# A hybrid decoder layer with PEER experts on one core: gathered rows broadcast by GpSimd, V sums over three PSUM banks, token weights in a zeroed wide row

## What is computed

```python
def _peer(h, wq, keys, u_tab, v_tab):                 # 288 tokens, width 2048
    q = (tb @ wq).reshape(TOK_BLOCK, PEER_HEADS, 2, PEER_DK)
    s = jnp.einsum('thpd,hpkd->thpk', q, keys)
    sv, si = lax.top_k(s, PEER_TOPK)
    ...                                               # the best 16 sums of two: eid (128 experts of a token), g (their weights)
    hid = jax.nn.gelu(jnp.einsum('td,ted->te', tb, u_tab[eid]), approximate=False)
    return jnp.einsum('te,ted->td', (g * hid), v_tab[eid])
```

## Time and profile before

| | |
|---|---|
| median of three runs | 2301.0 us |
| the profiled execution, its time | 2297.46 us |
| its span | 2295.3 us |
| TensorE (PE) busy | 2200.6 us, 96% |
| weight loads (PEld) busy | 1941.9 us, 85% |
| VectorE (DVE) busy | 1664.9 us, 73% |
| ScalarE (ACT) busy | 925.3 us, 40% |
| GpSimd (POOL) busy | 387.8 us, 17% |
| HBM traffic | 675.03 MB, mean 294 GB/s |
| chunks of gathered tokens run from, to | 1033 us to 2050 us |

### The profile page before, as it was taken

The page is one execution under the profiler, slowest core; times in us unless marked ns, Lnnn a source line. Parts: engine busy times, 40 slices in busy tenths (PEclk is TensorE's granted clock), DMA queues, the critical chain, the costliest instruction groups (busy, mean ns, idle before and its releaser), DMA issues.

```text
span 2295.3 us, 38685 instructions
## 1 busy us (share of the span) xinstructions
PE 2200.6 (96%) x14916; PEld 1941.9 (85%) x14916; DVE 1664.9 (73%) x3097; ACT 925.3 (40%) x1080; POOL 387.8 (17%) x336
## 2 busy tenths in 40 slices
PE   6899999779989999999999999999999999999996
PEld 2399888548979989999988888889888898989996
DVE  1269777434456699878888787887877878877686
ACT  1332323353353227644434444344343443444444
POOL 1044000300000008201122222222212322111000
PEclk9999999889999999999999999999999999999998
DMA  9977776976754445788899999998999999988863
GB/s 377 384 264 293 266 267 241 359 288 269 254 180 128 148 147 236 254 305 285 293 339 352 346 370 355 355 367 326 360 364 339 359 356 359 345 314 305 282 206 128
DMA packets 157366, 675.03 MB, mean 294 GB/s; under 512 B 17328, under 2 KB 17712, under 8 KB 134032
## 3 DMA queue, kind: packets, MB, share of 16 engines
q1 hardware_dynamic: 122112, 444.65, 54.2%
q0 software_dynamic: 33648, 219.49, 24.8%
q10 hardware_dynamic: 1440, 8.56, 0.9%
HBM read 650.68 MB, written 21.95 MB: 293 GB/s over the span
## 4 chain that ended last, share of the span: by engine, by line
PE 80%; DVE 8%; DMA 8%; ACT 2%; issue 1%; SPq 0%; DVEq 0%; POOL 0%; ACTq 0%
PE vb L1619 16%; PE zb L1604 14%; PE vb L1621 6%; PE zb L1606 6%; PE zb L531 5%; PE zb L533 5%; PE zb L532 5%; DMA ada_first<-in_w_ada 3%; PE vb L1653 3%; PE vb L1643 3%; PE vb L1584 2%; DMA raw<-in_v 2%; PE vb L1247 2%; DVE lo L484 2%; PE zb L1560 1%; PE zb L1247 1%
## 5 line engine op out<-in xcount | busy, mean ns | idle before, releaser
L475 ACT ACTIVATE hi<-raw 128x1024 fp32r<-128x1024 f32 x624 | 659.9, 1059 | 978.2 <-PE vb L1619 284.3
L484 DVE TENSOR_TENSOR lo<-raw,hi 128x1024 fp32r<-128x1024 f32 x624 | 765.7, 1231 | 276.2 <-ACT hi L475 267.9
L1604 PE MATMUL zb<-act_hl,hi 128*128 128x416 f32 x1792 | 556.5, 368 | 0.0
L1619 PE MATMUL vb<-w_rest,hi 128*128 128x416 f32 x1536 | 495.4, 368 | 0.0
L1606 PE MATMUL zb<-act_hl,lo 128*128 128x208 f32 x1680 | 435.6, 259 | 0.0
L1604 PEld LDWEIGHTS zb<-act_hl,hi 128*128 128x128 f32 x1792 | 335.1, 188 | 35.9 <-issue 27.7
L1621 PE MATMUL vb<-w_rest,lo 128*128 128x208 f32 x1280 | 329.9, 258 | 0.0
L1606 PEld LDWEIGHTS zb<-act_hl,lo 128*128 128x128 f32 x1680 | 320.8, 191 | 5.1
L1619 PEld LDWEIGHTS vb<-w_rest,hi 128*128 128x128 f32 x1536 | 288.8, 188 | 1.1
L531 PE MATMUL zb<-act_hl,hi 128*128 128x288 f32 x960 | 287.2, 299 | 0.0
L532 PE MATMUL zb<-act_hl,hi 128*128 128x288 f32 x960 | 282.5, 294 | 0.0
(11 more groups left out here) (291 smaller groups left out, 2759.1 us busy)
## 6 DMA issues: line engine op xcount, KB each, us to landing
raw<-in_v SPq DMA_DIRECT2D x256, 512.0 KB, 6.4
raw<-in_u SPq DMA_DIRECT2D x224, 512.0 KB, 6.4
raw<-in_w_in SPq DMA_DIRECT2D x80, 512.0 KB, 9.5
ada_first<-in_w_ada SPq DMA_DIRECT2D x64, 512.0 KB, 8.7
ada_mid<-in_w_ada SPq DMA_DIRECT2D x64, 512.0 KB, 5.3
ada_in<-in_w_ada SPq DMA_DIRECT2D x32, 512.0 KB, 8.8
raw<-in_w_out SPq DMA_DIRECT2D x32, 512.0 KB, 5.3
ada_last<-in_w_ada SPq DMA_DIRECT2D x32, 512.0 KB, 7.3
```

The costliest lines, as they stand in the source:

```text
L475: act.activation(hi[s][:, :], raw[s][:, :], ACT.Copy).then_inc(hi_ready, 1)
L484: dve.tensor_tensor(lo[s][:, :], raw[s][:, :], hi[s][:, :].bitcast(F32), ALU.subtract) \
L1604: last = pe.matmul(zb[:, bank, 0:2 * ND], w_h, act_hl[:, k, :, 0:ND], start=(k == 0), stop=(k == KC - 1))
L1619: last = pe.matmul(vb[:, bank, 0:2 * ND], v_h, w[:, e % 2, :, :], start=(e == 0), stop=(e == GI - 1))
```

## The change

- The rows of h of the gathered tokens are turned once (one transpose in place of two per block, no low parts, no tail) and stored to DRAM (`h_rows_d`, 80 x 2048). In the loop a half row (1024 numbers, 4 KB) is loaded into partition 0 by a DMA that ScalarE issues (row_load), 7 units ahead; GpSimd broadcasts it to 128 partitions with `partition_broadcast` (spread_half), 4 units ahead, into one of two buffers `h_wide`; VectorE's dot takes 1024 numbers with both inputs in SBUF. There are 160 halves in place of 320 chunks; half c stands at the unit of the old chunk 2c+1. TensorE has no part in it.
- Bank 3 of `vb` is free thereby, and the V sums rotate over three banks (0, 1, 3) in place of two.
- VectorE writes the weights of 8 tokens at once, 32 columns apart, in a row `w_wide` that GpSimd zeroed before the loop; a token's stationary matrix is a window of 32 columns of that row. The 80 instructions of `column` go.

```diff
@@ layout
-    return 53 * c // 48 - 8
+    return 53 * (2 * c + 1) // 48 - 8
+V_BANKS = (0, 1, 3)
+ROW_LEAD = 7
+SPREAD_LEAD = 4
-    h_rows = [at(f"h_rows{b}", [ROWS, 2, 512], F32R, (x_at + 14336, peer + 67968)[b]) for b in range(2)]
-    h_tail = at("h_tail", [P, 512], F32R, peer + 72064)
+    h_rows = [at(f"h_rows{b}", [NGT, 2, 512], F32, (x_at + 14336, peer + 67968)[b]) for b in range(2)]
+    h_wide = [at(f"h_wide{b}", [P, 1024], F32, (x_at + 14336, peer + 67968)[b]) for b in range(2)]
...
+        def h_row(c):
+
+            k = 8 * (c % 2)
+            return act_hl[0:1, k:k + 8, :, ND:ND + 64].bitcast(F32).rearrange("p k h d -> p (k h) d")
@@ gpsimd
-            pool.wait_ge(hs_turned, 1)
-            pool.tensor_copy(twice[:, :, :, :], hF[:, :, ND + NR:T].unsqueeze(2).to_broadcast([P, KC, 2, NT])) \
-                .then_inc(twice_ready, 1)
+            for b in range(2):
+                pool.wait_ge(hs_copied, b + 1)
+                pool.dma_start(h_rows_d[:, 1024 * b:1024 * b + 1024],
+                               h_rows[b][:, :, :].rearrange("t j d -> t (j d)")).then_inc(rows_out, 16)
+            def spread_half(c):
+
+                t, j = c // 2, c % 2
+                pool.wait_ge(row_in[j], 16 * t + 16)
+                if c >= 2:
+                    pool.wait_ge(dots_done, c - 1)
+                pool.partition_broadcast(h_wide[j][:, :], h_row(c), channels=P).then_inc(spread, 1)
+            pool.memset(w_wide[:, :], 0.0).then_inc(wide_zero, 1)
...
                 for n in range(32 * (g - 2), 32 * (g - 1)):
+                    for c in chunks_at(n + SPREAD_LEAD):
+                        spread_half(c)
                     for c in chunks_at(n):
-                        t = c // 4
-                        if c % 4 == 3 and t + 2 < NGT:
+                        t = c // 2
+                        if c % 2 and t + 2 < NGT:
                             pool.wait_ge(dots_done, c + 1)
                             gather(ug[t % 2], u_rows, t + 2, ug_in[t % 2])
@@ scalar
+            def row_load(c):
+
+                t, j = c // 2, c % 2
+                if t:
+                    act.wait_ge(spread, c - 1)
+                act.dma_start(h_row(c), h_rows_d[t:t + 1, 1024 * j:1024 * j + 1024].rearrange("t (k d) -> t k d", d=64))                     .then_inc(row_in[j], 16)
             def beside(n):
 
+                for c in rows_at(n):
+                    row_load(c)
@@ tensor
-                pe.wait_ge(w_col_ready, t + 1)
+                pe.wait_ge(w_s_ready, t // 8 + 1)
                 pe.wait_ge(vg_in[b], 8 * (t - b) + 16)
+                at_t = 31 + TS * (t % 16) - t % TS
                 for j in range(4):
-                    last = pe.matmul(vb[TS * j:TS * j + TS, 2, :], w_col[b][:, :], vg[b][:, 512 * j:512 * j + 512],
+                    last = pe.matmul(vb[TS * j:TS * j + TS, 2, :], w_wide[:, at_t:at_t + TS], vg[b][:, 512 * j:512 * j + 512],
                                      start=(t % TS == 0), stop=(t in BATCH_ENDS))
...
-                for c in chunks_at(n):
-                    spread_row(c)
                 for t in tokens_at(n):
                     value_token(t)
-                v_blocks(q, c, par, c % 2, 0, GI).then_inc(unit_used, 1)
+                v_blocks(q, c, par, V_BANKS[(KC * g + c) % 3], 0, GI).then_inc(unit_used, 1)
@@ vector
-            dve.sem_inc(vb_free, 2)
+            dve.sem_inc(vb_free, 3)
-                u = ug[b][:, 512 * j:512 * j + 512]
-                dve.tensor_tensor_reduce(u, u, vb[:, 3, :], 1.0, 0.0, ALU.mult, ALU.add, hid_4[:, c % 64:c % 64 + 1]) \
-                    .then_inc(dots_done, 1)
+                u = ug[b][:, 1024 * j:1024 * j + 1024]
+                dve.tensor_tensor_reduce(u, u, h_wide[j][:, :], 1.0, 0.0, ALU.mult, ALU.add,
+                                         hid_2[:, c % 32:c % 32 + 1]).then_inc(dots_done, 1)
...
-                for t in tokens_at(n + 2):
-                    column(t)
+                    places = w_wide[:, 31 + 256 * (i % 2):31 + 256 * (i % 2) + 8 * TS].rearrange("p (t x) -> p t x", x=TS)
+                    dve.tensor_tensor(places[:, :, 0:1], hid_s[:, 8 * i:8 * i + 8].unsqueeze(2),
+                                      gT[:, ND + 8 * i:ND + 8 * i + 8].unsqueeze(2), ALU.mult).then_inc(w_s_ready, 1)
```

More of the change, by code:

```diff
@@ L112, in chunks_at, with rows_at @@
 def chunks_at(n):
-    return [c for c in range(4 * NGT) if chunk_unit(c) == n]
+    return [c for c in range(2 * NGT) if chunk_unit(c) == n]
+def rows_at(n):
+    return [c for c in range(2 * NGT) if chunk_unit(c) - ROW_LEAD == n]
 def tokens_at(n):
@@ L122, in batches_at @@
 def batches_at(n, delay):
-    return [i for i in range(NGT // 8) if chunk_unit(32 * i + 31) + delay == n]
+    return [i for i in range(NGT // 8) if chunk_unit(16 * i + 15) + delay == n]
 ON_POOL = 2
@@ L199, in layer_kernel @@
     m_g5 = sb("m_g5", [P, KC, NC])
+    tmp_at = base[0]
     tmp_s = sb("tmp_s", [P, 2, TS])
@@ L299, in layer_kernel @@
     hid_s = at("hid_s", [P, NGT], F32, small_at + 384)
[L300 to L303, removed]
+    hid_2 = at("hid_2", [P, 32], F32, rs_at)
+    w_wide = at("w_wide", [P, 31 + 16 * TS], F32, rs_at + 256)
+    e_f = at("e_f", [P, NGT], F32, tmp_at)
     fin = at("fin", [P, KC, T], F32, x_at)
@@ L413, in layer_kernel @@
         hs_copied = sem("hs_copied")
-        hs_split = sem("hs_split")
-        twice_ready = sem("twice_ready")
+        rows_out = sem("rows_out")
+        row_in = [sem(f"row_in{r}") for r in range(2)]
         spread = sem("spread")
@@ L1032, in _ @@
                     for b2 in range(2):
[L1033 to L1039, removed]
+                        act.activation(h_rows[b2][:, :, :], vb[0:NGT, 2 * b2:2 * b2 + 2, :], ACT.Copy) \
+                            .then_inc(hs_copied, 1)
                 if j < KC // 2 - 1:
@@ L1071, in _ @@
             act.wait_ge(spilled, 16)
+            act.wait_ge(rows_out, 32)
+            for c in range(2):
+                row_load(c)
             for i in range(2):
@@ L1193, in _ @@
             round_w(2 * PP + 1, 1, 0)
+            for c in range(2, 4):
+                row_load(c)
             u_quad(Q_PEER + 10, 2, 2, 0)
+            row_load(4)
             u_quad(Q_PEER + 11, 2, 3, 0)
+            row_load(5)
+            row_load(6)
             for g in range(2, NG - 1):
@@ L1511, in _ @@
             for k in range(KC):
-                for r in (0, NR):
-                    last = pe.matmul(vb[r:r + NR, k // 4, P * (k % 4):P * (k % 4) + P], hF[:, k, ND:ND + NR], ident,
-                                     start=True, stop=True)
+                last = pe.matmul(vb[0:NGT, k // 4, P * (k % 4):P * (k % 4) + P], hF[:, k, ND:T], ident,
+                                 start=True, stop=True)
             last.then_inc(hs_turned, 1)
[L1517 to L1524, removed]
             pe.wait_ge(keys_in, 16)
             q_pair(2)
-            pe.wait_ge(hs_split, 2)
-            turn_tail()
+            pe.wait_ge(hs_copied, 2)
             key_scores(0)
@@ L1627, in v_unit @@
                 pe.wait_ge(lo_ready, 4 * q + c % 4 + 5)
-                v_blocks(q, c, par, c % 2, 0, GI).then_inc(unit_used, 1)
-            def spread_row(c):
-                if c == 0:
-                    pe.wait_ge(hs_copied, 3)
-                else:
-                    pe.wait_ge(dots_done, c)
-                t, j = c // 4, c % 4
-                if t < NR:
-                    one, rows = pick[:, t:t + 1], h_rows[j // 2][:, j % 2, :]
-                else:
-                    if c == 4 * NR:
-                        pe.wait_ge(hs_split, 3)
-                    one, rows = pick_tail[:, j, t - NR:t - NR + 1], h_tail[:, :]
-                pe.matmul(vb[:, 3, :], one.to_broadcast([P, P]), rows, start=True, stop=True).then_inc(spread, 1)
+                v_blocks(q, c, par, V_BANKS[(KC * g + c) % 3], 0, GI).then_inc(unit_used, 1)
             def value_token(t):
@@ L2301, in add_sums @@
                 dve.wait_ge(unit_used, 4 * q + c % 4 + 5)
-                sums = vb[:, c % 2, 0:2 * ND].rearrange("p (h t) -> p h t", h=2)
-                if isinstance(g, int) and g == 0:
+                sums = vb[:, V_BANKS[(KC * g + c) % 3], 0:2 * ND].rearrange("p (h t) -> p h t", h=2)
+                if g == 0:
                     dve.tensor_copy(acc[:, c, :, :], sums).then_inc(vb_free, 1)
```

67 lines of the change are left out of this document (21 added, 46 removed).

## The result

The changed kernel takes 2329.1 us (median of 4 runs, 2324.83 to 2334.76) against 2300.8 us before in the same runs: ratio 1.0116, 95% interval 1.0098 to 1.0134. It is 27 us slower, where 2249 us were forecast, 52 us faster; the time lies above the range (2218 to 2285 us) and on the other side of no change.

A forecast was written before the change was run, and what follows sets the result against it. TensorE, 96% busy, was taken as the bound, with DMA and VectorE close behind. Savings of 42 (long stretch) + 8 (short stretch) + 2.4 (query stage) - 0.5 (zeroing) = 52 us gave 2301 - 52 = 2249 us, range 2218 to 2285 us.

The forecast's parts named there:

- What leaves TensorE: 320 broadcast matmuls at 0.235 us leave TensorE: 59 us from 1240 to 2050 us, 16 us before that, 75 us in all.
- rival (a): Full gain: DMA speeds up, broadcasts hardly disturb VectorE, TensorE stays the bound; about 2222 us, chance 0.15.
- The added waits: ScalarE's row load waits for the broadcast two before; 1.8 units, some 5 us, were left for it, so no cost.
- rival (d): No change: the hand-overs make ScalarE wait 0.33 us at each of 160 row loads, giving back 52 us; 2301 us, chance 0.07.
- The port: GpSimd's broadcasts of 1.2 us hold up VectorE's two-SBUF-input operations, 0.8 of their length: 121 us in the long stretch.
- three floors: Long stretch, 1240 to 2050 us: TensorE 751, VectorE 747 to 777, DMA 741 to 761 us; 768 us taken.
- Rival (c): Slower: at 2.4 us a broadcast VectorE becomes the bound, decisive from 1.83 us; 2382 us, chance 0.13.
- DMA: In the long stretch the bytes stay the same; a floor of 741 to 761 us, by rates of 386 and 353 GB/s.
- Rival (b): DMA has no more to give: at a 360 GB/s ceiling the long stretch needs 794 us; 2275 us in all, chance 0.15.
- The wide row: Weights of 8 tokens in one zeroed row: set at nothing, as 10 small instructions change their stride alone.
- The third bank: A third bank for the V sums: set at nothing, only slack that the tighter long stretch can use.
- signs announced for a wrong forecast: `lo` at 1.22 us throughout, broadcasts over 1.8 us, ScalarE waiting for `spread`, or TensorE waiting at value tokens for V rows.

The follow-up runs named there:

- e9: e5 with every second token's V gather left out from token 3 on: 2229.2 us, ratio 0.9690 to the kernel before.
- e1: The changed kernel with all but the first two row loads left out, broadcasts kept: 2287.4 us, ratio 0.9932 to the kernel before.
- e3: The changed kernel with row loads issued 5 units ahead instead of 7 and broadcasts 3 instead of 4: 2282.6 us, ratio 0.9902 to the kernel before.
- e11: e3 with the V sums in two banks as before the change: 2288.9 us, ratio 0.9935 to the kernel before.
- e5: e1 with a GpSimd write of 8 columns in place of every broadcast from the third on: 2262.3 us, ratio 0.9833 to the kernel before.
- e13: e1 with a GpSimd write of all 1024 columns in place of every broadcast from the third on: 2245.6 us, ratio 0.9774 to the kernel before.
- e12: The kernel before with the wide zeroed row alone, no column instructions: 2300.3 us, ratio 0.9991 to the kernel before.
- e10: e3 with the first two broadcasts some 85 us earlier: 2283.3 us, ratio 0.9919 to the kernel before.
- e6: e3 with 64 in place of 128 rows per V gather: 2337.6 us, ratio 1.0161 to the kernel before.

## Why the prediction was wrong

**What leaves TensorE: right.** e9, with port, chain and part of the DMA load taken away, runs at 2229 us, 72 us under the kernel before; rival (a) said 2222. TensorE was busy for 2.89 us per `lo` unit in the long stretch before (806.5 us, 279 units) and for 2.66 us in e9 (801.9 us, 301 units): 63 us over 279 units, an estimate, where 59 were forecast. The 0.235 us per broadcast was about the right price of what TensorE gives up.

**The added waits: the step that failed.** The prediction found the chain, said that ScalarE had 1.8 units, 5 us, and set it at nothing; rival (d) had 0.07. Measured: 42 us (e1), or 49 us by e3 (1.0116 - 0.9902). The 1.8 units hold three errors. They are a mean of whole steps: between dot c-4 and row load c lie 2 units for 128 of the halves in the loop and 1 for 25. The broadcast was put in with 1.2 us, but takes 2.13 us when VectorE is at work, and starts only after a dot of 1.3 us; with one gather of 1.6 us that is already 5.0. And the count went by unit numbers, though each engine reaches a number at a time of its own: near 1611 us ScalarE was done with the `hi` copy before the load just when the dot ended, and nothing was left of the 5 us. Rival (d)'s price, a third of a microsecond for each of 160 loads, 52 us, was near the truth; its result, no change, was not, since port and DMA took the gain as well.

**The clock: a term that the sum lacks.** The prediction reads the full clock and keeps it. In the kernel after, pauses of TensorE were followed by stretches at a granted clock of 0.50, 26 us of work in all, against 12 in e1 and 7 in e3. So, at one for one, 14 (26 - 12) of the chain's 42 us could be clock, and 19 of the 49 by e3; e11 shows that it can be less. One traced execution of each kernel stands behind these counts. The waits stay the cause, as e1 and e3 remove the falls with them, but how much of their price is paid by the clock is open.

**The port: mechanism right, size and use wrong.** The broadcast alone takes 1.30 us; 1.2 was taken from the copy. Its hold on VectorE was put at 0.96 us each, 121 us in the long stretch. VectorE's operations grew by 272 x 108 ns for `lo` and 34 x 310 ns for `w_f`, 40 us, a third of that: the broadcast itself did most of the waiting, 1865 ns against 1300 in the mean. `lo` was announced at 1.4 to 1.6 us and came to 1.33. But the prediction then took the largest of three floors, 747 us for VectorE lying under 751, so that the port cost next to nothing. It cost 23 us (e1 to e5) to 36 us (e1 to e13). Rival (c) said slower, and slower it was, but by luck: its condition, broadcasts of over 1.83 us, was met (1.87), and what should follow from it wasn't, as VectorE is not full, 646 of 810 us. Its price of 2382 us rested on VectorE becoming the bound. (A small slip beside this: 216 less 209 us in the short stretch are 7 us saved, not 8.)

**DMA: near.** The 768 us taken lie 17 us over TensorE's own 751; e5 to e9 gives 33 us over the kernel, e13 to e9 19 us, with half of the V gathers away. That a higher rate can be had is shown by e13, 365 GB/s in its long stretch at share 0.95. Rival (b), a ceiling of 360 GB/s, falls with it.

**The rest.** The wide row at nothing: right (e12). The third bank at nothing: not refuted (e11).

**The sum, as the runs give it,** in ratios: TensorE alone 0.9690, DMA + 0.0143, port + 0.0099, chain + 0.0184, together 1.0116; by e13 DMA is + 0.0084 and the port + 0.0158. Each run is taken from the next, so the sum closes by construction; it doesn't show that the terms are independent of one another, and another order could divide them otherwise. The forecast of 2249 us is a ratio of 0.977: about that of e13 (0.9774), a kernel with neither port nor chain. That nearness is in part luck, as e5 has neither of them either and runs at 0.9833. Two of the signs announced for a wrong forecast were there: ScalarE waited for `spread`, and the broadcasts took over 1.8 us. What might have shown it in advance is a walk along one hand-over with the durations of contention: dot, broadcast behind a `lo`, gather, load.

## What to carry to other kernels

A wait added to an engine's queue is priced by what stands behind it, and its slack is counted in time, from the moment when the last instruction ahead ends on each engine, with the smallest distance and not the mean. Where the floors of three engines lie close together (here 751, 747 and 741 to 761 us), delays can add up, as they did here; the largest of the floors is not a forecast but its lower end. A pause of an engine can cost more than its length: look at the granted clock in short stretches behind it, since over 810 us the mean of 0.97 hides the level of 0.50. And before work is moved to GpSimd beside VectorE's operations on two SBUF inputs, ask whether it reads SBUF.

## What the hardware showed that was not expected

- A broadcast of 1024 floats to 128 partitions takes 1.30 us alone and 2.1 us (median) beside `lo` and dots. Ahead of the first one, behind its configuration instruction, GpSimd stood 8.6 us (5.9 us in e10, 10.8 us in e5):

```profile
L743 POOL PARTITION_BROADCAST h_wide<-act_hl x160: 1294/2129/2362, 1032.7 to 2070.7; - x160
L743 POOLq MODIFY_POOL_CONFIG  x2: 42/42/43, 1024.1 to 1024.2; - x2
...
  issue: 8.6, 1
```

- A gather of 64 rows to 64 partitions landed in 10.8 us (e6), one of 128 rows to 128 partitions in 10.3 us (e3; medians, 1240 to 2050 us), and with the smaller ones the kernel took 2338 us instead of 2283. The Trainium skill (SBUF — State Buffer, Door 1: The DMA port swizzle) has a transfer to partitions 0 to 63 use 8 of 16 ports. That agrees with the landing times: half the bytes, and no sooner there. Which ports were used was not read.
- A row load of 4 KB to one partition costs ScalarE's queue 0.49 us to issue and lands after 4.9 us.
- TensorE's granted clock fell to half behind a pause and stayed there for some microseconds: 0.50 from about 1553 to 1560 us after 3.65 us idle. Falls and missing clock (us of work, in stretches of 2 us from 1020 to 2080 us), beside TensorE's idle time from 1240 to 2050 us: before 0 falls, 0 us missing, 3.5 us idle; e9 0, 0, 8.1; e13 2, 3.4, 20.3; e5 3, 5.1, 33.7; e3 4, 6.8, 39.3; e1 5, 11.9, 44.8; after 9, 25.6, 57.4; but e11 9, 27.3, 38.9. So the idle time in all doesn't decide it alone.
